# Gated values stored whole and split in the down phase, sums on other engines, and a norm in place: one change to an encoder block on one NeuronCore

## The reference

```
h = rms_norm(x, mix_pre_g) * (1 + scale1) + shift1          # x: 2048 positions x 1024
... attention, Fourier mixing, gates, w_out ...
x = x + gate1 * rms_norm(y, mix_post_g)

h = rms_norm(x, ffn_pre_g) * (1 + scale2) + shift2
u = depthwise_conv_centred(h @ w_up, conv_w, conv_b)        # width 3 over positions, 2 x 2816 channels
a, bval = split(u, 2)
y = (gelu(a) * bval) @ w_down                               # 2816 -> 1024
x = x + gate2 * rms_norm(y, ffn_post_g)
```

## Time and profile before

| | |
|---|---|
| median of three runs | 3192.9 us |
| profiled execution | 3187.81 us, its span 3186.0 us |
| TensorE busy, share of span | 3059.6 us, 96% |
| VectorE | 2296.8 us, 72% |
| ScalarE | 1455.6 us, 46% |
| GpSimd | 658.3 us, 21% |
| granted TensorE clock, mean | 0.985 of full |

### The profile page before, as it was taken

One profiled execution on the slowest core, in us unless ns is written; L12 is line 12 of the kernel. 1 busy time (PEld: TensorE's weight loads), 2 busy tenths in 40 slices (PEclk: granted clock), 3 DMA queues, 4 the chain that ended last, 5 costly groups with the idle time before them and its releaser, 6 DMA issues.

```text
span 3186.0 us, 35637 instructions
## 1 busy us (share of the span) xinstructions
PE 3059.6 (96%) x13529; PEld 2451.5 (77%) x13529; DVE 2296.8 (72%) x2287; ACT 1455.6 (46%) x1793; POOL 658.3 (21%) x600
## 2 busy tenths in 40 slices
PE   7999999999999999999999799998999999998998
PEld 7777777777788888878888677776877877876777
DVE  5679677774699999986555788887443888884333
ACT  4433111112899999953333544444332444442222
POOL 0011431441000000000000344453202444440000
PEclk8999999999999999999999999999999999999999
DMA  8643333125611112266665222224774222326775
GB/s 324 215 146 128 127 109 111 68 79 182 171 34 37 37 34 57 69 188 208 212 200 193 97 107 107 106 107 148 255 250 149 106 106 106 108 109 240 245 253 171
DMA packets 173466, 454.26 MB, mean 143 GB/s; under 512 B 17992, under 2 KB 49736, under 8 KB 168808
## 3 DMA queue, kind: packets, MB, share of 16 engines
q1 hardware_dynamic: 155840, 400.07, 37.8%
q0 software_dynamic: 9968, 35.13, 3.0%
q10 hardware_dynamic: 7488, 16.78, 1.4%
HBM read 319.58 MB, written 127.09 MB: 140 GB/s over the span
## 4 chain that ended last, share of the span: by engine, by line
PE 23%; DVE 22%; issue 4%; POOL 3%; DMA 2%; ACT 2%; SPq 0%; DVEq 0%; ACTq 0%; POOLq 0%
DVE up_wu_lo L2325 6%; PE second_ps_b L90 4%; PE second_ps_b L91 4%; PE second_ps_b L92 4%; DVE ffn_cv L2767 4%; PE second_ps_a L90 3%; PE second_ps_a L91 3%; PE second_ps_a L92 3%; DVE ffn_cv L2765 3%; DVE ffn_cv L2772 2%; POOL ffn_u L2540 2%; ACT ffn_g_hi L2634 1%; DVE ffn_g_lo L2776 1%; DMA ffn_x<-scratch_x 1%; DVE ffn_u L2732 1%
## 5 line engine op out<-in xcount | busy, mean ns | idle before, releaser
L2780 DVE TENSOR_TENSOR ffn_wd_lo<-ffn_wd_st,ffn_wd_hi 128x1024 fp32r<-128x1024 f32 x110 | 130.0, 1221 | 286.5 <-ACT ffn_wd_hi L2648 286.5
L1525 DVE TENSOR_TENSOR att_prob_lo<-att_prob,att_prob_hi 128x1024 fp32r<-128x1024 f32 x256 | 310.0, 1221 | 23.9 <-ACT att_prob_hi L1484 22.8
L90 PE MATMUL second_ps_a<-up_in_hi,up_wu_hi 128*128 128x512 f32 x728 | 288.0, 396 | 16.5 <-DVE up_wu_lo L2325 14.9
L91 PE MATMUL second_ps_a<-up_in_lo,up_wu_hi 128*128 128x512 f32 x728 | 285.0, 392 | 0.0
L92 PE MATMUL second_ps_a<-up_in_hi,up_wu_lo 128*128 128x512 f32 x728 | 284.5, 391 | 0.0
L1484 ACT ACTIVATE att_prob_hi<-att_prob 128x1024 fp32r<-128x1024 f32 x256 | 272.3, 1064 | 0.0
L1478 ACT ACTIVATE att_prob<-att_ps_s 128x1024 f32<-128x1024 f32 x256 | 262.4, 1025 | 7.8 <-PE att_ps_s L1592 7.7
L2648 ACT ACTIVATE ffn_wd_hi<-ffn_wd_st 128x1024 fp32r<-128x1024 f32 x110 | 110.8, 1052 | 319.9 <-PE second_ps_a L92 163.1
L920 ACT ACTIVATE proj_out<-proj_ps,proj_bg 128x512 f32<-128x512 f32 x64 | 44.1, 689 | 379.5 <-PE proj_ps L92 365.5
L90 PE MATMUL second_ps_b<-up_in_hi,up_wu_hi 128*128 128x512 f32 x504 | 199.4, 396 | 11.8 <-DVE up_wu_lo L2325 6.5
L1997 POOL DMA_DIRECT2D scratch_x<-second_y x16 | 9.9, 618 | 956.6 <-DVE second_y L2171 956.6
(11 more groups left out here) (330 smaller groups left out, 8264.6 us busy)
## 6 DMA issues: line engine op xcount, KB each, us to landing
ffn_wd_st<-in_w_dn SPq DMA_DIRECT2D x110, 512.0 KB, 4.8
up_w_st<-in_w_up SPq DMA_DIRECT2D x88, 512.0 KB, 4.3
ffn_g_ring<-scratch_g SPq DMA_DIRECT2D x88, 384.0 KB, 4.0
scratch_gates<-proj_out SPq DMA_DIRECT2D x64, 256.0 KB, 2.0
early_w_st<-in_w_branch SPq DMA_DIRECT2D x32, 512.0 KB, 6.2
merge_gate<-scratch_gates SPq DMA_DIRECT2D x64, 256.0 KB, 3.4
scratch_g<-ffn_g_hi SPq DMA_DIRECT2D x22, 512.5 KB, 2.7
scratch_g<-ffn_g_lo SPq DMA_DIRECT2D x22, 512.5 KB, 3.6
```

The source lines that it names most:

```text
L90: pe.matmul(out, w_hi, x_hi, start=first, stop=False)
L91: pe.matmul(out, w_hi, x_lo, start=False, stop=False)
L1525: dve.tensor_tensor(prob_lo[:, s % LAG, :], prob[:, s % RING, :], prob_hi[:, s % LAG, :], ALU.subtract)\
L2780: dve.tensor_tensor(wd_lo[:, m % 4, :], wd_st[staged_at(m)][:], wd_hi[:, m % 4, :], ALU.subtract).then_inc(s_dlo, 1)
```

## The change

- `store_g` stores g itself, once, in place of its two parts; `load_g` loads it into one buffer `g_raw`, and `high_g(n)` and `low_g(n)` split it per group n in the down part into the ring `gs`.
- The product P5 is no more copied by ScalarE. VectorE makes `u4 = P5 + u2` (into the row of a) and `c22 = P5 + u3` from PSUM; `c12` adds to the row in place. The bank of P5 is free after `c22`.
- GpSimd keeps only the four weight sums in the up passes; they get a buffer of their own (`own`, `owns`) from the third pass of a half on (the second in the second half).
- The two edge columns of the convolution are copied by ScalarE in `tap`, not by VectorE.
- VectorE's order in a pass is new: `low(i, LAST)` stands behind both convolutions, `low(i+1, S12)` ahead of `c12`. SP loads group 1's g ahead of the store of the half's last g.
- The norm scales the tile in PSUM in place, then adds it into `x1`, which has four slots and is stored from there. TensorE waits for the sum (`s_o`) where it waited for the scaling (`s_n`).

```diff
-        self.sums34 = at("w_sums34", [P, 2, BLK], 192 * kib + 32, F32)
+        self.own = at("w_sums_own", [P, 4, BLK], 188 * kib, F32)
...
+    def owns(self, i, g):
+
+        return i % NP >= self.OWN_ROOM or i == NP + 1 or i == NP and g == self.S34
...
-        if o in (self.S1, self.S2) or i < self.OWN_ROOM:
+        if not self.owns(i, self.GROUP_OF[o]):
             self.room(pool, i, self.GROUP_OF[o])
-        else:
-            pool.wait_ge(self.s_lo, self.GROUPS * (i - 1) + self.S34 + 1)
+        elif i > self.OWN_ROOM:
+            pool.wait_ge(self.s_lo, self.GROUPS * (i - 1) + self.GROUP_OF[o] + 1)
...
-        if g == self.S12:
+        if g == self.S12 and not self.owns(i, g):
             dve.wait_ge(self.s_sum, 4 * i + 4)
...
-    gs = [at(f"g_ring{v}", [P, 2, 2, BLK], (196 * kib + 64, 88 * kib)[v], F32R) for v in range(2)]
-    yw = at("yw", [P, 2, D], 168 * kib)
-    x1 = at("x1", [P, 2, D], 176 * kib + 64)
+    g_raw = at("g_raw", [P, 2, BLK], 192 * kib)
+    gs = [at(f"gs{v}", [P, 2, 2, BLK], (88 + 8 * v) * kib, F32R) for v in range(2)]
+    x1 = at("x1", [P, 4, D], 168 * kib)
...
-    S_TAKEN = (s_p1, s_p5, s_u2, s_c11, s_u3, s_c12, s_c21)
...
+    S_TAKEN = (s_p1, s_c22, s_u2, s_c11, s_u3, s_c12, s_c21)
...
-            sp.wait_ge(s_glo, i + 1)
-            for part, g in enumerate((g_hi[v], g_lo[v])):
-                sp.dma_start(g_d[c, part, :, to:to + many], g[:, first:first + many].bitcast(F32)).then_inc(s_gst[v], 16)
+            sp.wait_ge(s_g, i + 1)
+            sp.dma_start(g_d[c, :, to:to + many], g_at(i)[:, first:first + many]).then_inc(s_gst[v], 16)
...
+            b = n // GR
+            if n == first_group(half):
+                sp.wait_ge(wu.s_lo, wu.GROUPS * (NP * (half + 1) - 1) + wu.S34 + 1)
+            else:
+                sp.wait_ge(s_glo, n)
             for a in range(2):
-                sp.wait_ge(s_gst[a], 32 * ((NP // 2) * half + gr + 1))
+                sp.wait_ge(s_gst[a], 16 * ((NP // 2) * half + gr + 1))
             first, many = BLOCKS[b][0] * P, len(tiles(b)) * P
             for a in range(2):
-                sp.dma_start(gs[v][:, a, :, 0:many].bitcast(F32),
-                             g_d[2 * gr + a, :, :, first:first + many].rearrange("h p s -> p h s")).then_inc(s_gl[v], 16)
+                sp.dma_start(g_raw[:, a, 0:many], g_d[2 * gr + a, :, first:first + many]).then_inc(s_gl, 16)
...
-            load_dn(2 * first_group(half) + 2)
-            load_dn(2 * first_group(half) + 3)
+            load_pair(first_group(half) + 1)
+            load_g(first_group(half) + 1)
             store_g(last)
-            load_g(first_group(half) + 1)
-            sp.wait_ge(s_gst[1], 32 * (NP // 2) * (half + 1))
...
-        def take_u4(i):
-            pool.wait_ge(s_p5, i + 1)
-            pool.wait_ge(s_u3, i + 1)
-            pool.tensor_tensor(u2[:], u2[:], p5[:], ALU.add).then_inc(s_u4, 1)
-
-        def take_c22(i):
-            if i == NP:
-                pool.wait_ge(s_o, LAST_TILE[0] + 1)
-            elif i:
-                pool.wait_ge(s_cd, 2 * i)
-            pool.tensor_tensor(u[:, 1, 2 + BLK:2 + HALF], u3[:], p5[:], ALU.add).then_inc(s_c22, 1)
...
-        def copy_p5(i):
-            act.wait_ge(s_up, wu.MANY * i + P5 + 1)
-            if i:
-                act.wait_ge(s_u4, i)
-                act.wait_ge(s_c22, i)
-            act.activation(p5[:], bank_of(i, P5), ACT.Copy).then_inc(s_p5, 1)
...
+            if i >= NP:
+                act.wait_ge(s_keep, 2 * NP)
+                act.activation(u[:, j, 0:2], carry[:, c, :], ACT.Copy).then_inc(s_halo, 1)
+                act.wait_ge(s_halo, 2 * (i - NP) + j + 1)
+            act.activation(cv[:, j, :], u[:, j, 0:NCV], ACT.Identity, bias=cw[:, c, 3:4], scale=cw[:, c, 0:1]).then_inc(s_tap, 1)
             if i < NP:
...
+        def high_g(n):
+            v, many = ring(n), len(tiles(n // GR)) * P
+            act.wait_ge(s_gl, 32 * (n + 1))
...
+            if n - first_group(half) >= 2:
+                act.wait_ge(s_dn, down_done(n - 1))
+            act.activation(gs[v][:, :, 0, 0:many], g_raw[:, :, 0:many], ACT.Copy).then_inc(s_ghi, 1)
...
+        def take_u4(i):
+            dve.wait_ge(s_up, wu.MANY * i + P5 + 1)
+            dve.wait_ge(s_u2, i + 1)
+            if i:
+                dve.wait_ge(s_cd, 2 * i - 1)
+            if i == NP:
+                for v in (2, 3):
+                    dve.wait_ge(s_ost[v], stored(v, LAST_TILE[0] + 1))
+            if i:
+                dve.wait_ge(s_keep, 2 * min(i, NP) - 1)
+            dve.tensor_tensor(u[:, 0, 2 + BLK:2 + HALF], bank_of(i, P5), u2[:], ALU.add).then_inc(s_u4, 1)
+
+        def take_c22(i):
+            dve.wait_ge(s_u3, i + 1)
+            if i:
+                dve.wait_ge(s_cd, 2 * i)
+                dve.wait_ge(s_keep, 2 * min(i, NP))
+            dve.tensor_tensor(u[:, 1, 2 + BLK:2 + HALF], bank_of(i, P5), u3[:], ALU.add).then_inc(s_c22, 1)
...
-            dve.tensor_tensor(u[:, 0, 2 + BLK:2 + HALF], bank_of(i, P3), u2[:], ALU.add).then_inc(s_c12, 1)
+            dve.tensor_tensor(u[:, 0, 2 + BLK:2 + HALF], bank_of(i, P3), u[:, 0, 2 + BLK:2 + HALF], ALU.add).then_inc(s_c12, 1)
...
+        def low_g(n):
+            v, many = ring(n), len(tiles(n // GR)) * P
+            dve.wait_ge(s_ghi, n + 1)
+            dve.tensor_tensor(gs[v][:, :, 1, 0:many], g_raw[:, :, 0:many], gs[v][:, :, 0, 0:many], ALU.subtract).then_inc(s_glo, 1)
...
-            if uses(t):
-                dve.wait_ge(s_ost[in_ring(t)], 16 * uses(t))
+            wide = g2[:].rearrange("p (c q) -> p c q", q=BLK)
             if t < NT - 1:
-                dve.scalar_tensor_tensor(at, down_of[spot].rearrange("p c q -> p (c q)"), rstd[:, t:t + 1], g2[:], ALU.mult, ALU.mult)\
-                    .then_inc(s_n, 1)
+                dve.scalar_tensor_tensor(down_of[spot], down_of[spot], rstd[:, t:t + 1], wide, ALU.mult, ALU.mult).then_inc(s_n, 1)
                 dve.wait_ge(s_n, t + 1)
-                dve.wait_ge(s_x[in_ring(t)], 16 * (uses(t) + 1))
-                dve.tensor_tensor(at, at, x1[:, in_ring(t), :], ALU.add).then_inc(s_o, 1)
+                dve.wait_ge(s_x[v], 16 * (uses(t) + 1))
+                at = x1[:, v, :].rearrange("p (c q) -> p c q", q=BLK)
+                dve.tensor_tensor(at, down_of[spot], at, ALU.add).then_inc(s_o, 1)
...
                 take_c21(i - 1)
+                convolve(i - 1, 0)
+                convolve(i - 1, 1)
                 wu.low(dve, i, wu.LAST)
-                convolve(i - 1, 0)
-                if half:
-                    halo(i, 0)
-                convolve(i - 1, 1)
-                if half:
-                    halo(i, 1)
                 times(i - 1)
-            elif half:
-                halo(i, 0)
-                halo(i, 1)
             if i == 0:
                 th.low(dve, 0, th.T3)
                 th.low(dve, 0, th.B22)
             take_u2(i)
-            if c:
-                low_g(i - 1)
-            take_c11(i)
+            take_u4(i)
             if i == 0:
                 th.low(dve, 0, th.T4)
                 norm2.mean_of_rows(dve, LB)
             more = c < NP - 1
+            n = first_group(half)
             if more:
                 wu.low(dve, i + 1, wu.A)
             else:
-                low_dn(2 * first_group(half))
+                low_dn(2 * n)
+            take_c11(i)
             take_u3(i)
-            if not more:
-                low_dn(2 * first_group(half) + 1)
+            take_c22(i)
+            if more:
+                wu.low(dve, i + 1, wu.S12)
+            else:
+                low_dn(2 * n + 1)
             take_c12(i)
             if more:
-                wu.low(dve, i + 1, wu.S12)
                 wu.low(dve, i + 1, wu.S34)
+            else:
+                low_g(n)
...
                 if k == 0:
                     take_c21(last)
+                    low_dn(2 * n + 2)
                     convolve(last, 0)
+                    low_dn(2 * n + 3)
                     convolve(last, 1)
-                    low_dn(2 * n + 2)
+                    low_g(n + 1)
                     times(last)
-                    low_dn(2 * n + 3)
-                    low_g(last)
                     dve.wait_ge(s_g2, 16 * (half + 1))
                 elif n + 1 in groups(half):
                     low_dn(2 * n + 2)
                     low_dn(2 * n + 3)
+                    low_g(n + 1)
...
-                pe.wait_ge(s_n, 4 + n // 2)
+                pe.wait_ge(s_o, 4 + n // 2)
...
-            pe.wait_ge(s_gl[v], 32 * (before_in_ring(n) + 1))
+            pe.wait_ge(s_glo, n + 1)
```

More of the change, by code:

```diff
@@ L2279, in sum_of @@
     def sum_of(self, i, o):
-        if o in (self.S3, self.S4) and i >= self.OWN_ROOM:
-            return self.sums34[:, o - self.S3, :]
-        return self.sums[:, o, :]
+        return self.own[:, self.SUMS.index(o), :] if self.owns(i, self.GROUP_OF[o]) else self.sums[:, o, :]
     def source(self, i, g):
@@ L2286, in source @@
```

(50 more changed lines are left out.)

157 lines of the change are left out of this document (71 added, 86 removed).

## The result

The changed kernel takes 3244.6 us (median of four runs, 3240.3 to 3245.2) where the kernel before takes 3192.9 in the same session: ratio 1.0163, 95% interval 1.0145 to 1.0181. It is slower by 51.6 us and lies above the range of the prediction (3190, range 3166 to 3211). The profiled execution has a span of 3243.2 us, 57.2 more than before.

What follows compares the result with a forecast made beforehand. VectorE's loop, not TensorE, was taken to set the up passes. -5 + 12.5 - 7.5 + 12 + 1 - 14.5 - 1 = -2.5 us on 3187.8 gave 3185.3; against the median 3190, range 3166 to 3211.

Steps and rivals of the forecast that it cites:

- The loop: Up passes: with low(LAST) behind both convolutions, the chain from weight load to next low(LAST) lengthens each pass from 19.85 to 20.65 us.
- the other term, 5.65: Up pass: time from low(LAST) to GpSimd's first weight sum, 5.65 us; upper bound assumed weights landing 0.5 us later.
- Exclusion of VectorE and GpSimd: Up pass: the two engines take turns; low(S12) goes first by 0.09 us, so GpSimd's fourth sum ends at 7.06 us.
- Rival 1: Up passes: fourth sum slips in ahead of low(S12), or weights land earlier; pass 20.1 us, 20 us less, 3170; chance 0.15.
- rival 3: Up passes: the loop doesn't bind; passes at 19.05 us, 59 us less, 3131; chance 0.1.
- The bank of the second product: Up, first half: bank held until c22, so product 1 starts at t + 7.0 instead of 5.95 us, once, not per pass.
- Up, first half: First up phase: 18 passes x 0.8 less TensorE's 2 us lead, +12.5 us; separately -5 at the start.
- Up, second half: Second up phase: -4 for its first pass, then 19 passes x 0.85 = +16; together +12 us.
- -4 for the first pass: Second up phase: TensorE's 3.7 us wait in its first pass goes, as low(S12) waits neither for c12 nor u4.
- Beginning of the down phase: Start of each half's down part: -7.5 us first half, +1 second, including a 4.1 us stop before the second half's third group.
- Block ends: Down part: four x1 slots and in-place PSUM scaling remove norm waits that stop TensorE; -14.5 us, bounds -8 and -15.
- the theory that came true: Up passes: chain longer than laid out, store of g close behind weights; pass 21.2 us, 20 us more, 3210; chance 0.2.

Runs made afterwards that it cites:

- experiment 1: Changed kernel with one line moved: VectorE's split of the last matrix, low(LAST), ahead of both convolutions again; 3137.4 us, ratio 0.9839.
- experiment 9: Changed kernel, own order, store of g issued only when both weight transfers landed, first four x1 loads of each half two groups later; 3194.8 us, ratio 1.0025.
- experiments 2 and 9: First: changed kernel, SP waits until both weight transfers have landed before issuing the store of g, 3204.2 us, ratio 1.0047. Second: see experiment 9.
- experiments 4 and 5: First: kernel before, low(LAST) moved behind both convolutions, 3283.3 us, ratio 1.0298. Second: changed kernel, low(LAST) between the two convolutions, 3136.8 us, ratio 0.9845.

## Why the prediction was wrong, point by point

**The loop.** Right in its layout: `low(LAST)` behind the convolutions makes a loop of the weight loads that no engine's load explains. From the first sum to `low(LAST)` 14.9 us, forecast 14.95. The step that failed is the other term, 5.65, taken unchanged from the earlier trace rows and allowed at most 0.5 more. It measured 6.70, since the store of g follows the weights by 0.8 us. At 1 us a pass this is 37 us by the ratios and 40.4 by the medians and by the up phases of the traces, some three quarters of the loss. The trace of before could have warned me: its weight transfers take up to 5.3 us in single cases, so 0.5 more was no bound. A smaller slip: the same pass was put at +0.8 in the first half and at +0.85 in the second.

**Exclusion of VectorE and GpSimd.** Right: `low(S12)` ahead of the fourth sum, which takes 2.30 us. Rival 1 (pass 20.1) and rival 3 (the loop doesn't bind) didn't come.

**The bank of the second product.** Forecast as a shift of product 1, once. TensorE in fact waits for `c22` in nearly all passes of the first half, but for no more than it would wait for the loop anyway: without the loop (experiment 1) no stop is left.

**Up, first half.** Forecast 12.5 from the passes and -5 at the start. With the store held back the stretch is 474.1 us long, 12.4 more than before; 2.9 of these are the stop at its end, which the forecast counts in the down phase, so 9.5 against 7.5. After the change TensorE comes out of the transposes 2.0 us earlier than before, not 5. In experiment 1, where the loop doesn't bind, it is 6.7 us: a gain at the start is lost where the loop binds at once.

**Up, second half.** Forecast -4 for the first pass; wrong in sign. Before, the first two `low(LAST)` of this half are 17.04 us apart, since the loop had slack; after, 20.86. A wait of TensorE that goes gives nothing where the loop behind it is already the longer. With the store held back the stretch is 17.5 us longer than before, 3.5 of them the stop at its end, so 14.0 where I had 12.

**Beginning of the down phase.** The first stop was right (2.6 and 3.9 us of "issue" for 3.1 and 4.1). The stop before the third group was forecast in the second half alone, at 4.1 us, from SP's queue; it measured 6.2 and 11.7 us. The step that failed: I counted what SP had queued, and not GpSimd's four loads of `x1`, which the change doubles. Holding them back takes the stops to 2.2 and 6.6 us (experiment 9). The whole is worth 7 us by the ratios of experiments 2 and 9 (9.4 by the medians of the two sessions, 5.9 in the down phases of the traces), since part of it comes back as the new stop.

**Block ends.** Right in the main: the waits of the earlier trace rows for stores and for `x1` are gone, and of the stops of 5.5 + 4.5 us 3.8 are left. From the start of the third group to the end of each down phase it is 5.0 and 8.2 us less than before. Forecast -14.5, and -1 for the tail.

**The sum.** The trace after is 59.7 us longer than forecast (3245.0 for 3185.3). With the stops at the end of the up phases counted in the down phases, as the forecast does, 44.3 of them lie in the up phases (40.4 the store), 9.0 between the end of an up phase and the third group of the down phase, 2.3 at block ends and in the tail, and 4.0 ahead of the feed-forward part, which the change doesn't touch. By the ratios: 3190.4 forecast + 10.5 (what experiment 9 still misses) + 7.0 (x1) + 37.0 (store) = 3244.9, against 3244.6 measured. Of what experiment 9 misses, its trace has 5 us in the up phases, 6.6 at block ends, most of them in the second half with its stop of 4.18 us, and 3.4 ahead of the feed-forward part. The chances: the theory that came true had 0.2, with an effect half as large as it then had. The range ended 34 us too low: a pass of 21.2 was its worst and 21.6 came, some 16 us, and the beginnings of the down phases, 9 us, had no rival at all.

## What to carry to other kernels

When a step moves, draw the loop that it joins, and ask for each transfer in that loop what else is then in flight, on any queue and also behind it: a store that "costs nothing" on an idle queue can lie on top of the load that all wait for. Look at the order of the instructions on the loop's path first, and then at the waits: here one line decided between 1.6% slower and 1.6% faster, and the sum of the loop told in advance where it lets go. Loads that become possible earlier, because there are more buffers, should be issued when they are needed, not when they can be.

## What the runs showed of the hardware

In the steady up passes two 0.5 MB loads are issued 0.4 us apart. A 0.5 MB store issued 0.8 us behind the second makes it land 1.0 us later (5.5 for 4.5 us), from SP's or ScalarE's queue alike, and takes 6.1 us itself instead of 2.6 to 3.0. Issued 3.5 us behind (experiments 4 and 5), it does nothing to the load. A second store right behind the first adds 0.13 us. The Trainium skill ("DMA: Bandwidth & Descriptors", Two DMAs through the same engine are not ordered) says that descriptors of one queue of a DMA engine start in order but are pipelined; I had drawn from the order that a later transfer is harmless, and it isn't. When 5.5 MB are asked for within 6 us, the loads of `w_dn` and g, whose medians over the changed kernel are 4.7 and 4.2 us, take 9.8 and 10.7.
